# S5 stage of a hybrid flow-matching step: sixteen gate bands, not eight, ahead of the sixteen batches

## What is computed

```python
proj = h @ lw["w_in"]
q, k, v, r, glr, u, lx, ly, gates = jnp.split(proj, _in_splits(), axis=-1)
...
x_re = jnp.einsum("bcgi,gpi->bcgp", u_c, bb_re)
x_im = jnp.einsum("bcgi,gpi->bcgp", u_c, bb_im)
...
_, _, h_re, h_im = lax.associative_scan(_complex_combine, (a_re, a_im, x_re, x_im), axis=1)
y = jnp.einsum("bcgp,gip->bcgi", h_re, c_re) - jnp.einsum("bcgp,gip->bcgi", h_im, c_im)
...
g_gla, g_s5, g_lru = jnp.split(jax.nn.sigmoid(gates), 3, axis=-1)
```

## Time and profile before

| what | us |
|---|---|
| median of 3 runs | 2937.99 (2936.61 to 2940.48) |
| the profiled execution's own time | 2935.89 |
| its span, first to last instruction | 2934.1 |
| PE busy | 2795.7 (95%) |
| DVE busy | 1782.6 (61%) |
| ACT busy | 1137.6 (39%) |
| POOL busy | 932.4 (32%) |
| the S5 stage in the span | about 957 to 1511 |

### The profile page before, as it was taken

How to read it: one execution, slowest core, us unless ns; L and a number is a source line. 1 busy time by engine, 2 the same in 40 slices (tenths; PEclk the granted TensorE clock), 3 DMA queues, 4 the chain that set the end, 5 groups by cost and what they waited for, 6 DMA issues and landing times. The chain is left out here.

```text
span 2934.1 us, 41574 instructions
## 1 busy us (share of the span) xinstructions
PE 2795.7 (95%) x16768; PEld 2735.7 (93%) x16768; DVE 1782.6 (61%) x2422; ACT 1137.6 (39%) x1709; POOL 932.4 (32%) x624
## 2 busy tenths in 40 slices
PE   6999999999999998999969999999999999999996
PEld 6999998899998998999969999999999999999996
DVE  7688886364454899999954547778732223223226
ACT  2698995352643314444441101013642211211224
POOL 1334433111211265555514334333112111111223
PEclk9999999999999999999989999999999999999998
DMA  6121112011201544444443546434111111111111
GB/s 229 45 65 61 60 60 62 28 37 40 58 24 43 152 149 146 122 123 123 116 160 133 184 133 218 139 133 139 37 44 44 38 42 44 44 44 44 44 44 65
DMA packets 111179, 257.80 MB, mean 88 GB/s; under 512 B 20960, under 2 KB 54752, under 8 KB 110752
## 3 DMA queue, kind: packets, MB, share of 16 engines
q1 hardware_dynamic: 100928, 214.26, 23.3%
q10 hardware_dynamic: 10080, 41.18, 3.8%
HBM read 199.01 MB, written 56.37 MB: 87 GB/s over the span
## 5 line engine op out<-in xcount | busy, mean ns | idle before, releaser
L153 POOL TENSOR_TENSOR w_lo<-w_raw,w_hi 128x256 fp32r<-128x256 f32 x292 | 343.2, 1205 | 716.8 <-ACT w_hi L205 507.6
L2691 PE MATMUL bank<-yhi,w_hi 128*128 128x384 f32 x1560 | 525.0, 337 | 3.7 <-POOL w_lo L2621 2.3
L2691 PE MATMUL bank<-ylo,w_hi 128*128 128x384 f32 x1560 | 521.8, 335 | 0.0
L2691 PE MATMUL bank<-yhi,w_lo 128*128 128x384 f32 x1560 | 521.7, 334 | 0.0
L2621 POOL TENSOR_TENSOR w_lo<-w_raw,w_hi 128x1024 fp32r<-128x1024 f32 x69 | 169.1, 2451 | 678.4 <-ACT w_hi L2799 678.4
L2658 PE MATMUL bank<-yhi,w_hi 128*128 128x384 f32 x864 | 290.8, 337 | 27.5 <-POOL w_lo L197 22.6
L2691 PEld LDWEIGHTS bank<-yhi,w_hi 128*128 128x128 f32 x1560 | 293.2, 188 | 7.4 <-POOL w_lo L2621 3.3
L2691 PEld LDWEIGHTS bank<-ylo,w_hi 128*128 128x128 f32 x1560 | 293.4, 188 | 1.1
L2691 PEld LDWEIGHTS bank<-yhi,w_lo 128*128 128x128 f32 x1560 | 293.4, 188 | 0.0
L2658 PE MATMUL bank<-yhi,w_lo 128*128 128x384 f32 x864 | 289.6, 335 | 0.0
L2658 PE MATMUL bank<-ylo,w_hi 128*128 128x384 f32 x864 | 289.6, 335 | 0.0
(11 more groups left out here) (453 smaller groups left out, 6575.8 us busy)
## 6 DMA issues: line engine op xcount, KB each, us to landing
w_raw<-in_mlp_units SPq DMA_DIRECT2D x64, 512.0 KB, 3.6
w_raw<-in_s_units SPq DMA_DIRECT2D x32, 512.0 KB, 4.6
mrg_scr<-in_w_ada_rows SPq DMA_DIRECT2D x32, 512.0 KB, 3.7
mid_gates<-gate ACTq DMA_DIRECT2D x24, 576.0 KB, 3.3
gt<-mid_gates SPq DMA_DIRECT2D x24, 576.0 KB, 3.8
w_raw<-in_gla_units SPq DMA_DIRECT2D x25, 512.0 KB, 3.7
w_raw<-in_lru_units SPq DMA_DIRECT2D x24, 512.0 KB, 3.6
x<-in_x_t SPq DMA_DIRECT2D x16, 576.0 KB, 9.5
```

The costliest lines, as they stand in the source:

```text
L153: ins = pool.tensor_tensor(lo[:, part], raw[:, part], hi[:, part].bitcast(F32), ALU.subtract)
L2691: mm = pe.matmul(out, wt[SLOT[u]][:, w], r[:, k, band_cols(b)], start=(k == first and y == 0), stop=(k == last and y == 2))
```

## The change

`LEAD` becomes 16, so eight more gate bands are computed ahead of batch 0. To have 72 in all, batches 6 to 13 take three bands in place of four (14 and 15 had three already); the pass after the last batch keeps its two. SP loads the weights of units 13, 14 and 15, which those bands and the next need, in its queue ahead of the batches: unit 13 before `store_tab(3)`, units 14 and 15 behind it.

```diff
-        LEAD = 8
+        LEAD = 16
...
-            per = [4 if k < 14 else 3 for k in range(LAST)] + [0]
+            per = [4 if k < 6 else 3 for k in range(LAST)] + [0]
...
                 load_unit(UNITS_U + 4)
+                load_unit(UNITS_U + 5)
                 store_tab(3)
+                load_unit(UNITS_U + 6)
+                load_unit(UNITS_U + 7)
                 sync.wait_ge(tab_out[1], 64)
```

## The result

The changed kernel takes **2945.24 us** (median of 14 runs, 2942.96 to 2947.94) against 2939.74 for the kernel before in the same comparison (14 runs, 2931.43 to 2944.39). The ratio is **1.0024, 95% interval 1.0017 to 1.0031**: slower by 5.5 us, just past what can be told from no change. The profiled execution took 2946.32 us, 10.4 more than that of before. Of these, 7.5 arose in the S5 stage (`outputs(15)` starts at 1506.55, before at 1499.03); the other 2.8 lie behind it, where nothing was changed (1437.9 us from there to the end of the span, before 1435.1). These are two single executions; the medians differ by 5.5 us, less than the stage does between the two.

A forecast was written before the change was run, and what follows sets the result against it. PE and DVE were taken as full at the same pace, with DVE the bound after the change. Terms summed to -0.5 to +1.1, plus half a us for alignment: +1, 2939.0 us, own range 2935 to 2943, wide range 2932 to 2947.

The forecast's parts named there:

- Lead to 1117.3: Before batch 0: without waits the lead starts from 1084.0, adds eight bands of 4.16 us and ends at 1117.3.
- wait at `transposes(1)`: Batch 1 on PE: a new wait of 1.2 to 2.3 us for `input_weights(1)`, taken as 1.3.
- The weights of unit 12: In the lead: ready by 1096.4 to 1097.8, first band at 1099.7, two us of slack, cost nothing.
- Rival C: Lead not hole-free: unit 12 or `transposes(1)` 2 to 4 us later, moving DVE by all of it; 2942, chance 0.1.
- First batch: DVE from `states(0)` to `states(1)`: 18.2 + 0.45 x about 11 = 23.2 us, `states(1)` at 1142.7.
- the prediction's own price: DVE beside POOL, throughout the batches: 0.45 us of DVE lost per us of POOL.
- Batches 1 to 5: Four bands as before, 24.9 us each on PE and DVE: 124.5 us, `states(6)` at 1267.2.
- the alignment: Batches 6 to 13: split beside DVE's PSUM reads costs 0.7, not 2.0; batch 22.9 to 23.0, not 24.2; 24.0 taken.
- the sign that I had named: From about batch 8: PE waits of 2 to 3.5 us before each `lag_blocks` on DVE, 15 to 20 in all.
- Rival D: The alignment holds from batch 8 on, 22.9 us for six batches: -6, 2933, chance 0.15.
- the prediction's chain: PE from batch 14's lag: 1.9 + 4.2 + 3.1, then 2.2 and 8.4; `lag_blocks(15)` at 1479.0 to 1480.6.
- rival B: DVE gains nothing from thinner batches, 24.9 us each, and its 13.3 us late start is kept: +8, 2946, chance 0.15.

The follow-up runs named there:

- twelve bands: LEAD = 12 against the kernel before's 8, four bands in each of the first ten batches, `input_weights(1)` before the lead's last split; 0.9968, again 0.9978.

## Why the prediction was right in kind and short in size

**What bounds.** Shown: DVE is a second bound, found from the absence of waits, at the same pace as PE, and it is the only one in batches of three.

**Lead and DVE's start.** Lead to 1117.3, measured 1117.92; wait at `transposes(1)` 1.3, measured 1.2; `states(0)` at 1119.5, measured 1120.15. The weights of unit 12 cost nothing, as said. Rival C does not hold.

**First batch: the term that was mis-sized.** I had 11 us of POOL beside DVE and `states(1)` at 1142.7; it was 18.7 us, and 1146.2. POOL's timeline shows what I left out:

```profile
1118.28 1.06 POOL L1783 TENSOR_TENSOR wtr<-pwwr,bbr 128x512 f32<-128x512 f32 x1
...
1123.97 1.66 POOL L1788 TENSOR_TENSOR wti<-wti,wtmp 128x512 f32<-128x512 f32 x1
1132.54 4.93 POOL L153 TENSOR_TENSOR w_lo<-w_raw,w_hi 128x256 fp32r<-128x256 f32 x4 [6.91 <-ACT w_hi L205]
1137.43 1.57 POOL L1783 TENSOR_TENSOR wtr<-pwwr,bbr 128x512 f32<-128x512 f32 x1
...
1145.42 1.69 POOL L1788 TENSOR_TENSOR wti<-wti,wtmp 128x512 f32<-128x512 f32 x1
```

A tail of `input_weights(1)`, a split, and then all of `input_weights(2)`, which falls wholly on `output_weights(1)`. One of its instructions:

```profile
1138.00 1.61 DVE L2263 TENSOR_TENSOR catmp<-pqi,cci 128x576 f32<-128x576 f32 x1
```

Such an instruction takes 0.76 us where POOL is idle. With 18.7 us of POOL the prediction's own price gives 18.2 + 8.4 = 26.6, against 26.1 measured: the price was right and the count wrong, by 2.9 us of DVE. The kernel without `input_weights(2)` shows it (23.4).

**Batches 1 to 5.** 124.5 forecast, 125.7 measured: +1.2.

**Batches of three.** The sum without the alignment gave 24.2, and 24.26 was measured, 194.1 for the eight. I took 24.0 for a favourable place of the split behind slot 1; nothing of it is in the average of the changed kernel: +2.1. It was argued, not read from a row. That single batches differ shows in the 22.1 to 25.7 us above, but on average they gained nothing. With it goes the sign that I had named, 2 to 3.5 us of wait before each `lag_blocks` from batch 8 on: the sum of 16.5 lies in the range of 15 to 20, but it comes in five waits of 0.6 to 4.7, with none before `lag_blocks(11)` and `(13)`. Rival D fails.

**The end.** `states(14)` came at 1465.99, not 1459.2. PE's timeline at `lag_blocks(14)`, where DVE let it go, and at `outputs(15)`, and the window behind the first:

```profile
1465.53 0.64 PE L1873 MATMUL bank<-ca0r,bblk0r 128*32 128x128 f32 x2 [4.53 <-DVEq L2268]
...
1506.55 0.58 PE L1887 MATMUL bank<-ub,wia 128*128 128x144 f32 x1 [1.98 <-DMA wia<-mid_kd]
```
```profile
1465.50:1468.90 3.40, 3.37 (x16) 2.67 (x16) 2.76 (x5) 0.00 (x0) 1.19 (x2) 0.51 0.67 176
```

From there the prediction's chain fits: 3.4 us of lag blocks at half clock, 4.2, 3.1, 2.2 and 8.4 give 1486.8 for `lag_blocks(15)`, measured 1487.0. In the kernel before, DVE had finished `output_weights(14)` well before PE came to `lag_blocks(14)`, as the timelines of DVE and PE show:

```profile
1453.20 0.76 DVE L2264 SCALAR_TENSOR_TENSOR ca0i<-ca0i,catmp 128x576 f32<-128x576 f32 x1
...
1459.65 0.41 PE L1870 MATMUL bank<-ca0r,bblk0r 128*32 128x128 f32 x2
```

That slack of 5.7 us is why 11.5 us on DVE (1465.99 against 1454.53) became 7.5: 11.5 - 5.7 + 1.5 for the clock is 7.3. It is also why twelve bands gain more than DVE does: `states(15)` comes 4.0 us earlier (1470.6), `outputs(15)` 8.2 (1490.82).

**The sum.** +1 forecast, +7.5 measured in the stage, 6.5 too little. The terms: 0.6 of the lead's end, 2.9 of the first batch, 1.2 and 2.1 of the next two stretches, together 6.8 at `states(14)`; behind it the chain held. The size is that of rival B (+8), but not by its mechanism: a thin batch did gain (24.26, not 24.9 or 24.6). The medians give +5.5. I had given slower past 0.2% only 0.16; the 1.0024 lies there, if barely. The 2945.24 is past my own range (2935 to 2943) and lies only in the wide one, which was stretched to 2947 for rival B; so that it fits is luck as to the size. The engine that bounds and the lost start were not luck.

## What to carry to other kernels

When no view shows a wait of a second engine, count that engine's start and its total work as a bound of their own: filling holes of the first engine with work ahead of the loop pays only up to the moment when the second is ready to begin. Here that was twelve bands with POOL's item in the right place, 0.997 to 0.998; beyond it a band costs up to what it takes, less what it lifts off the loop. And when work is shifted, recount for each stretch what a third engine now does beside the bound one: the price per us held in every trace within 0.02, the count did not.

## What the runs showed of the hardware

**DVE beside POOL.** Eleven traces give 0.43 to 0.45 us lost on DVE per us of POOL, over 151 to 217 us of it. POOL pays too: its instruction at L1783 takes 1.06 us while DVE stands idle, and 1.57 beside `output_weights(1)`. The loss is not even: the four products read from PSUM stay at 0.75 us beside POOL, while the six instructions of `output_weights(1)` took 8.9 us beside `input_weights(2)`, 4.5 alone, and there one instruction of DVE and one of POOL both take about 1.6 us.

The Trainium skill, "SBUF — State Buffer", section "SBUF: two separate sides", has the loser of the shared port pair blocked for the whole instruction, but of DVE's instructions it names only those with two inputs in SBUF (and the two-port modes). My reading in the prediction left this condition out. With it the PSUM reads are no exception to the page; the trace agrees there (0.75 us), and in `output_weights(1)` the 1.6 us come near to one instruction of each in turn (0.76 and 1.06). Averaged over whole batches the loss is smaller, 0.45.

**The clock behind short waits.** PE's waits of 2.25 us (`lag_blocks(8)`) and 0.58 us (`lag_blocks(9)`), and the clock behind each:

```profile
1322.18 0.64 PE L1873 MATMUL bank<-ca0r,bblk0r 128*32 128x128 f32 x2 [2.25 <-DVEq L2268]
...
1345.17 0.41 PE L1873 MATMUL bank<-ca1r,bblk1r 128*32 128x128 f32 x2 [0.58 <-DVEq L2268]
```
```profile
1322.20:1325.60 3.40, 3.40 (x16) 2.65 (x16) 3.17 (x5) 0.02 (x1) 3.40 (x5) 0.50 0.83 268
1345.20:1348.60 3.40, 3.40 (x25) 3.20 (x26) 3.17 (x5) 2.95 (x9) 2.46 (x4) 1.00 0.91 243
```

Behind the first the granted clock is 0.50 (1.2 GHz) and the lag blocks take 3.4 us instead of 1.9; behind the second it is 1.00 (2.4 GHz). The length of a wait of this size does not settle it. Two in the first trace with twelve bands, ahead of `lag_blocks(12)` and `(13)`, and the clock behind them:

```profile
1405.43 0.41 PE L1871 MATMUL bank<-ca0r,bblk0r 128*32 128x128 f32 x2 [2.25 <-DVEq L2266]
...
1428.45 0.42 PE L1871 MATMUL bank<-ca1r,bblk1r 128*32 128x128 f32 x1 [2.26 <-DVEq L2266]
```
```profile
1405.40:1408.80 3.40, 3.37 (x25) 3.17 (x26) 3.11 (x5) 1.36 (x5) 3.40 (x5) 1.00 0.93 297
1428.40:1431.80 3.40, 3.35 (x16) 2.66 (x16) 3.09 (x5) 0.08 (x1) 3.40 (x5) 0.51 0.84 235
```

In all thirteen traces, between the lead and `outputs(15)`, no wait of PE of 0.4 to 1.6 us was followed by the slow stretch, every one of 3.0 us or more was, and those of 2.0 to 2.3 us (the one at `outputs(15)` among them) went either way. In the middle of the stage the slow stretch costs nothing, since DVE is late anyway; behind `lag_blocks(14)` it cost its full 1.5 us.
